# Attention of a hybrid decoder layer: masks behind a step's products, and both branches of a head in a row

## The reference, cut to what matters

```
s = einsum('bgrqd,bgnd->bgrqn', qi, ck) * scale            # compressed keys, 63 blocks
p_c = masked_softmax(s, cmp_end[None, :] <= t[:, None])
...
s = einsum('bgrqd,bgqkd->bgrqk', qi, ksel) * scale         # selected blocks of 64 keys
p_s = masked_softmax(s, smask[:, :, None])                 # key <= token
...
s = einsum('bgrqd,bgkd->bgrqk', qi, kwi) * scale           # window of 512 keys
p_w = masked_softmax(s, wmask)
...
o = gates[..., 0:1] * o_c + gates[..., 1:2] * o_s + gates[..., 2:3] * o_w
```

## Time and profile before

| | |
|---|---|
| median of 3 runs | 1591.72 us (1591.71 to 1593.87) |
| profiled execution | 1593.65 us |
| its span (first to last instruction) | 1591.9 us, 1.75 outside it |
| mean granted TensorE clock | 0.991 of 2.4 GHz |
| attention, about | 366 to 652 us of the span |
| of it token tiles 0 to 3 (steps 0 to 7) | 366.0 to 468.7 us |

### The profile page before, as it was taken

The page is one execution under the profiler, slowest core; times in us unless marked ns, Lnnn a source line. Parts: engine busy times, 40 slices in busy tenths (PEclk is TensorE's granted clock), DMA queues, the critical chain, the costliest instruction groups (busy, mean ns, idle before and its releaser), DMA issues.

```text
span 1591.9 us, 21511 instructions
## 1 busy us (share of the span) xinstructions
PE 1556.8 (98%) x8238; PEld 1264.0 (79%) x8238; DVE 894.6 (56%) x1561; ACT 536.8 (34%) x936; POOL 78.4 (5%) x126
## 2 busy tenths in 40 slices
PE   7999999998999999999999999999999999999997
PEld 6888888897666666788888888888888888888885
DVE  7832455446777777443455555656555555556332
ACT  6112222246677777422222211222112221223221
POOL 0111222220000000000000000000000000000000
PEclk9999999998999999999999999999999999999998
DMA  6433243380000000601211111121111111122011
GB/s 229 134 105 127 93 146 102 111 261 18 24 18 14 15 1 15 237 1 44 76 40 60 59 40 40 40 79 40 40 40 57 62 40 40 40 80 106 27 40 40
DMA packets 53239, 110.57 MB, mean 69 GB/s; under 512 B 13104, under 2 KB 22320, under 8 KB 53168
## 3 DMA queue, kind: packets, MB, share of 16 engines
q1 hardware_dynamic: 45744, 85.47, 16.2%
q0 software_dynamic: 7424, 24.12, 4.5%
HBM read 89.65 MB, written 19.92 MB: 69 GB/s over the span
## 4 chain that ended last, share of the span: by engine, by line
PE 95%; DVE 2%; issue 2%; ACT 1%; DMA 0%; DVEq 0%; POOLq 0%; POOL 0%; SPq 0%; ACTq 0%
PE ps L1521 29%; PE ps L1140 15%; PE ps L1142 15%; PE ps L1141 15%; PE ps L1247 6%; PE ps L1426 5%; PE ps L1383 3%; PE ps L1384 2%; PE ps L1508 1%; PE ps L1292 1%; PE ps L1240 1%; PE ps L1145 1%; PE ps L1387 1%; PE ps L1206 1%; PE ps L1381 0%
## 5 line engine op out<-in xcount | busy, mean ns | idle before, releaser
L2070 DVE TENSOR_TENSOR h<-h,ps 128x512 f32<-128x512 f32 x336 | 224.3, 686 | 137.9 <-PE ps L1142 136.2
L1521 PE MATMUL ps<-hth,wuh 128*128 128x512 f32 x672 | 206.9, 389 | 0.0
L1521 PE MATMUL ps<-htl,wuh 128*128 128x512 f32 x672 | 206.9, 389 | 0.0
L1521 PE MATMUL ps<-hth,wul 128*128 128x512 f32 x672 | 206.8, 389 | 0.0
L1140 PE MATMUL ps<-wh,xth 128*128 128x512 f32 (+1 forms) x448 | 175.4, 392 | 8.0 <-DVE wl L1655 8.0
L1142 PE MATMUL ps<-wh,xtl 128*128 128x512 f32 (+1 forms) x448 | 169.4, 378 | 0.0
L1141 PE MATMUL ps<-wl,xth 128*128 128x512 f32 (+1 forms) x448 | 168.9, 377 | 0.0
L1521 PEld LDWEIGHTS ps<-htl,wuh 128*128 128x128 f32 x672 | 126.1, 188 | 26.2
L1521 PEld LDWEIGHTS ps<-hth,wuh 128*128 128x128 f32 x672 | 126.1, 188 | 26.2
L1521 PEld LDWEIGHTS ps<-hth,wul 128*128 128x128 f32 x672 | 126.1, 188 | 26.2
L1084 ACT ACTIVATE ffh<-ffa 128x1024 fp32r<-128x1024 f32 x22 | 23.3, 1061 | 358.3 <-DVE ffa L2097 358.3
(11 more groups left out here) (249 smaller groups left out, 2593.0 us busy)
## 6 DMA issues: line engine op xcount, KB each, us to landing
wuraw<-in_w_up SPq DMA_DIRECT2D x44, 512.0 KB, 5.1
wraw<-in_w_in SPq DMA_DIRECT2D x48, 256.0 KB, 3.4
proj_d<-stage POOLq DMA_DIRECT2D x48, 256.0 KB, 2.3
wdraw<-in_w_down SPq DMA_DIRECT2D x22, 512.0 KB, 3.5
rin<-proj_d POOLq DMA_DIRECT2D x20, 256.0 KB, 4.6
xraw<-in_xt SPq DMA_DIRECT2D x16, 256.0 KB, 5.6
owraw<-in_w_out SPq DMA_DIRECT2D x8, 512.0 KB, 5.8
h<-in_x SPq DMA_DIRECT2D x1, 4096.0 KB, 16.8
```

The source lines that it names most:

```text
L1521: mm = nc.tensor.matmul(ps[:, 2 * part + half, :], w_, x_[:, k, half * 512:(half + 1) * 512], start=(k == 0 and i == 0), stop=(k == NK - 1 ...
L2070: nc.vector.tensor_tensor(hh, hh, ps[:, 4 + o_ % 4, :], ALU.add).then_inc(dn_add, 1)
```

## The change

1. The row of products and masks is split in two functions: `qk_products` issues all products of a unit, `qk_masks` behind them the masks. In tiles 4 to 7 the far mask thus comes behind the joint products, with the diagonal and the compressed mask.
2. In tiles 0 to 3 (`late`, `paired`) PE computes both branches of a head in a row in every second slot: products of both, then masks of both (`qk_pair`). The DVE takes both row maxima at the start of the even slot, ACT both exponentials at the end of the odd slot.
3. In these tiles, which need one bank a unit, units use two sets of banks: selected scores bank 0 or 1, window scores bank 2 or 3, by the head's parity (`score_bank`). A unit waits for exponentials four units back (`apart`). Unit 1 waits for those of the whole step before (its compressed scores use bank 3), unit 3 for `csub_done` of its own step.
4. For steps 0 to 7 the transposes, outputs and `close` start one slot later; for steps 6 and 7 they are packed in 7 slots, so that they end where they ended.

```diff
+        def late(v):
+            return v < G * WIN_T
+        def paired(v):
+            return late(v)
...
-                base = per * (v + 1) + 1
+                base = per * (v + 1) + (2 if late(v) else 1)
+                span = per - 1 if late(v) and not late(v + 2) else per
...
-                    slots[base + per * at // total].extend(unit)
+                    slots[base + span * at // total].extend(unit)
...
-                slots[base + per - 1].append(("close", v))
+                slots[base + span - 1].append(("close", v))
...
+        def apart(t):
+            return 4 if t < WIN_T else 2
+        def score_bank(t, i):
+            r_, br = divmod(i, 2)
+            return 2 * br + (r_ % 2 if t < WIN_T else 0)
...
+            def exp_places(n, length):
+                v, i = divmod(n, 2 * RG)
...
+                if late(v):
+                    return {length: [i - 1, i]} if i % 2 else {}
+                if not paired(v):
+                    return {length: [i]}
...
-            def qk(v, i):
+            def qk_products(v, i):
...
-                if n >= 2:
+                if n >= apart(t):
+                    pe.wait_ge(exp_done, n - apart(t) + 1)
+                if i == 1 and t < WIN_T and n >= 2:
                     pe.wait_ge(exp_done, n - 1)
                 if i == 1 and v:
                     pe.wait_ge(csub_done, CSUB0 + v)
+                if i == 3 and t < WIN_T:
+                    pe.wait_ge(csub_done, CSUB0 + v + 1)
+                if i == 2 and v == 0:
+                    pe.wait_ge(cvc_done, CVC0 + 1)
...
+            def qk_masks(v, i):
+                t, (r_, br) = v // G, divmod(i, 2)
+                far = br and t >= WIN_T
+                at = (t - (max(0, t - WIN_T) if br else 0)) * P
+                if far:
+                    nc.tensor.matmul(ps[:, 2, 0:P], ident_b[:], far_b, start=False, stop=True)
+                mm = nc.tensor.matmul(ps[:, score_bank(t, i) + at // 512, at % 512:at % 512 + P], ident_b[:], diag_b,
+                                      start=False, stop=not far)
+                if far:
+                    c0 = P + r_ * HD
+                    mm = nc.tensor.matmul(ps[:, 3, c0:c0 + HD], ident_b[:], cmp_b[:, t], start=False, stop=True)
                 mm.then_inc(qk_done, 1)
+            def qk(v, i):
+                qk_products(v, i)
+                qk_masks(v, i)
+            def qk_pair(v, r_):
+                for br in range(2):
+                    qk_products(v, 2 * r_ + br)
+                for br in range(2):
+                    qk_masks(v, 2 * r_ + br)
...
-            qk(0, 0)
+            qk_pair(0, 0)
...
-                if n + 1 < 2 * RG * NV:
-                    qk(*divmod(n + 1, 2 * RG))
+                v_, i = divmod(n + 1, 2 * RG)
+                if v_ < NV and not paired(v_):
+                    qk(v_, i)
+                elif v_ < NV and i % 2 == 0:
+                    qk_pair(v_, i // 2)
...
-                if n < 2 * RG * NV:
-                    row_max(*divmod(n, 2 * RG))
+                u_, i = divmod(n, 2 * RG)
+                if u_ < NV and not paired(u_):
+                    row_max(u_, i)
+                elif u_ < NV and i % 2 == 0:
+                    row_max(u_, i)
+                    row_max(u_, i + 1)
```

More of the change, by code:

```diff
@@ L939, in exponentials @@
                     act.wait_ge(tr_full, turns_of["turn_p", v - 2, len(key_tiles(v - 2)) - 1] + 1)
-                s_, pr = ps[:, 2 * br:2 * br + 2, :].rearrange("p a n -> p (a n)"), prob[:, v % 2, r_]
+                at = score_bank(t, i)
+                s_, pr = ps[:, at:at + 2, :].rearrange("p a n -> p (a n)"), prob[:, v % 2, r_]
                 m, q = n % 4, n // 2 % 4
@@ L981, in nsa_high @@
                                      ps[:, 7, 0:2 * P].rearrange("p (a n) -> p a n", a=2), ACT.Copy).then_inc(nsah_done, 1)
+            def exp_places(n, length):
+                v, i = divmod(n, 2 * RG)
+                if v >= NV:
+                    return {}
+                if late(v):
+                    return {length: [i - 1, i]} if i % 2 else {}
+                if not paired(v):
+                    return {length: [i]}
+                if i % 2:
+                    return {}
+                if i == 0:
+                    return {length: [0, 1]}
+                return {(length + 1) // 2: [i], length: [i + 1]} if length > 1 else {length: [i, i + 1]}
             for e in range(2):
@@ L1006, in _ @@
             for n, slot in enumerate(slots):
-                for st in slot:
+                at_ = exp_places(n, len(slot))
+                for m, st in enumerate([*slot, ("end",)]):
+                    for i in at_.get(m, ()):
+                        exponentials(n // (2 * RG), i)
                     {"split_q": q_split_high, "turn_q": q_turned, "turn_p": p_high, "turn_ret": ret_high,
                      "close": nsa_high}.get(st[0], skip)(st)
-                if n < 2 * RG * NV:
-                    exponentials(*divmod(n, 2 * RG))
                 if n in OW_SLOTS:
@@ L1366, in qk @@
                     w = min(512, width - c)
-                    bank = 2 * br + c // 512
+                    bank = score_bank(t, i) + c // 512
                     at = w0 * P + c
[L1369 to L1375, removed]
+                    if br and c:
                         two = ps[:, 3:5, :].rearrange("p a n -> p (a n)")[:, 0:2 * c0].rearrange("p (b n) -> p b n", b=2)[:, :, 0:P]
@@ L1380, in qk @@
                             pair = bass.AP(k_, first, [[CK + 3 * HD, P], [gap, 2], [1, P]])
-                            mm = nc.tensor.matmul(two, q_, pair, start=k_ is keys_s, stop=False)
+                            nc.tensor.matmul(two, q_, pair, start=k_ is keys_s, stop=False)
                     else:
+                        ends = c + w < width and not br
                         nc.tensor.matmul(ps[:, bank, 0:w], q_, aks[:, br, g_, at:at + w], start=True, stop=False)
[L1384 to L1389, removed]
+                        nc.tensor.matmul(ps[:, bank, 0:w], q_, akx[:, br, g_, at:at + w], start=False, stop=ends)
                 if i == 1 and t < WIN_T:
@@ L1395, in qk @@
                         nc.tensor.matmul(sc_, qc, ckx[:, g_ * NCMP:g_ * NCMP + HD], start=False, stop=False)
-                        mm = nc.tensor.matmul(sc_, ident_b[:], cmp_b[:, t], start=False, stop=True)
-                mm.then_inc(qk_done, 1)
+                        nc.tensor.matmul(sc_, ident_b[:], cmp_b[:, t], start=False, stop=True)
+            def qk_masks(v, i):
[9 more added lines that the diff above has]
+                    mm = nc.tensor.matmul(ps[:, 3, c0:c0 + HD], ident_b[:], cmp_b[:, t], start=False, stop=True)
+                mm.then_inc(qk_done, 1)
+            def qk(v, i):
[6 more added lines that the diff above has]
+                    qk_masks(v, 2 * r_ + br)
             def p_turn(st):
@@ L1891, in row_max @@
                 m = n % 4
-                s_ = ps[:, 2 * br:2 * br + 2, :].rearrange("p a n -> p (a n)")
+                at = score_bank(t, i)
+                s_ = ps[:, at:at + 2, :].rearrange("p a n -> p (a n)")
                 if br == 0:
@@ L1900, in row_max @@
                 c_ = cmpst[:, v % 2]
-                scores = s_[:, 5 * P:5 * P + RG * HD].rearrange("p (r n) -> p r n", r=RG)[:, :, 0:NCMP]
+                scores = ps[:, 3, P:P + RG * HD].rearrange("p (r n) -> p r n", r=RG)[:, :, 0:NCMP]
                 maximum = mark(nc.vector.reduce_max(c_[:, C_MAX], scores, AX_X, negate=True))
```

## The result

The changed kernel takes 1599.70 us at the median of 22 executions (1593.67 to 1601.61), the kernel before 1593.47 us (22 executions, 1590.67 to 1595.33): ratio 1.0032, 95% interval 1.0024 to 1.0041 (the ratios here weigh all executions and lie near the quotient of the means, not of the medians). It is **slower by 0.3%**; the forecast was 1591.0 us and the range ended at 1598.0.

The account below looks back on a forecast made before the run. TensorE, busy 98% of the span, was taken as the bound. Terms -2.3 (steps 0 to 7) + 3.0 (clock) + 0.5 (step 8) - 2.0 (masks) = -0.8 us from 1591.72 gave 1591.0 us, range 1584.5 to 1598.

Parts of the forecast that it names:

- One sign of being wrong: Listed as refuting: steps 6 and 7 not longer, clock in steps 4 to 7 below 1.00, tiles 4 to 7 changing over 3 us.
- One sign of being right: Listed as confirming, among others: steps 0 to 3 shorter by 3 us or more together.
- Wait A: Step's head: head 0's window product waits for all exponentials of the step before; PE stands 1.8 us in step 7.
- Wait B: Head 1's window product waits for the compressed maximum's subtraction: 0.3 us in steps 6 and 7, about 1.6 in 3 to 5.
- Steps 4 to 7: Token tiles 2 and 3, one step per head group: 61.0 against 57.4 us, 3.6 us lost at full clock.
- Steps 0 to 3: Token tiles 0 and 1, DVE sets the pace: 39.4 against 45.3 us, 5.9 won, 3 given back to the clock.
- Step 8's head: Later transposes take 1.6 us of cover from step 8's start: 0.5 us lost, bounds 0 and 1.6.
- Masks last in tiles 4 to 7: Far mask behind the joint products hides 0.08 us of weight load per head: 2.0 us won, bounds 0 and 2.6.
- That holds at 2.4 GHz throughout: Assumption behind the net 2.3 us won in steps 0 to 7; only steps 0 to 3 got a clock correction, 3 us.
- the third rival: Holes at PE pull the clock down in steps 4 to 7: 9 us lost, 1600; if half, 1596; chance 0.22.
- the cases without it: Gains given back (0.38), denser early steps keep the clock (0.35), window-exponential wait at step heads costs nothing new (0.05).
- point of decision: The clock loss in steps 4 to 7 decides once a second low-clock stretch appears, each some 2 us.

Follow-up runs that it names:

- holes_filled: Changed kernel with selected products repeated on PE ahead of the four long waits in steps 4 to 7; 1591.90 us, ratio 0.9989.
- masks_only: Changed kernel with only the masks behind the products kept; no pairs, second set of banks or later slot; 1591.31 us, ratio 0.9994.
- t01_filled: Changed kernel with pairs in token tiles 0 and 1 alone, plus repeated products in the holes of steps 0 to 3; 1589.02 us, ratio 0.9971.
- pairs_t01: Changed kernel with pairs, two sets of banks and later transposes in token tiles 0 and 1 alone; 1590.66 us, ratio 0.9983.
- t01_shift: `pairs_t01` with four repeats of the first unit's products at the head of attention; 1591.47 us, ratio 0.9987.
- shift_1us: Changed kernel with four repeats of the products at attention's very first unit, 0.9 us later; 1601.90 us, ratio 1.0058.
- shift_2us: Changed kernel with eight repeats of the products at attention's very first unit, 1.2 us later; 1602.35 us, ratio 1.0060.
- no_later: Changed kernel with start and spread of the transposes, outputs and close as before the change; 1606.65 us, ratio 1.0089.
- mask_first: Changed kernel with head 0 of a step not paired, its mask right behind its selected products; 1597.25 us, ratio 1.0017.

## Why the prediction was wrong

Forecast 1591.0 us, measured 1599.70, and slower, which had a chance of 0.28. Of the 8.7 us between, 1.75 were in the start: the forecast began at 1591.72, the median of three executions, and 22 give 1593.47 for the same kernel. Beside that the time moved by +6.2 us instead of -0.8. One sign of being wrong stood in the first profile already: a clock below 1.00 in steps 4 to 7 (0.87 in step 4). One sign of being right was missing: steps 0 to 3 won 1.2 us, not 3 or more. Step by step, by the profiles:

- **Wait A**: 1.8 us in step 7 and 1.6 in step 6 were forecast, 1.75 and 1.53 came. Right.
- **Wait B**: 1.7 and 1.6 us in steps 4 and 5 were forecast, 1.61 and 1.60 came; in steps 6 and 7, where 0.3 was forecast, no wait of its kind shows. In step 3 1.6 was forecast and 1.45 came. Right.
- **Steps 4 to 7**: 12.25, 13.3, 15.45 and 20.0 us were forecast, 13.3, 12.6, 14.9 and 19.4 came: 61.0 against 60.2 us. That this is near is in part luck. The forecast was for a clock of 1.00, and step 4's low stretch is in the 60.2. In `holes_filled`, at 1.00, these steps take 58.5 us (409.87 to 468.42). The written order was priced some 2.5 us too high.
- **Steps 0 to 3**: 5.9 - 3.0 = 2.9 us won forecast, 1.2 measured. The clock is the suspect: the forecast took 3 us for 18 us at the low level, 0.17 each. The changed kernel has 0.77 over 44.1 us, 20 us at the low level, and `masks_only` against before suggests 0.32 each, 6.4 us. That is too much to fit (39.4 + 6.4 = 45.8, measured 44.1). `t01_filled` against `pairs_t01` gives at least 1.6 us for some 10 us, 0.16 each, with the repeats' own work in it. How the 1.7 us too few divide between the clock and the written order isn't shown.
- **Step 8's head**: 0.5 forecast, 0.4 measured (a wait of 1.02 us, as written out). Right.
- **Masks last in tiles 4 to 7**: 2.0 forecast, 1.7 measured, and 0.12 us between the joint products as forecast. The row of 0.20 beside 0.12 us spoke rightly.
- **The step that failed** is the clock in steps 4 to 7 ("That holds at 2.4 GHz throughout"). The forecast's sum took it as 1.00 there, on the ground of rows 2 (step 4 with PE idle 2 of 13.1 us at 1.00). Instead 3.2 to 10 us at 1.2 GHz follow waits A and B, and without these holes the time is 1591.9 us instead of 1599.70. That idle time was in pieces: the longest wait of PE from 410 to 470.5 us before is 0.9 us, in `t01_shift` 1.1 us, and both keep 1.00. Less idle time, but in one piece of 1.6 us, did not keep it in step 4 of the changed kernel. The piece alone isn't the whole rule: before, in steps 0 to 3, 20 us ran at the low level with no wait over 0.9 us. I had written down the pieces' length, and the third rival with it, and still weighed the share of idle time more: 0.22 for the rival against 0.78 for the cases without it.

What the rival said of its size: 9 us, or half of it, 1596 to 1600. The groups are some 6 us apart. The low stretches shown are 3.2 to 6.6 us long in `shift_1us` and 10 us in `shift_2us`. By the 1.6 us that 3.5 us cost in step 4, that is an estimate of 1.5 to 4.6 us each; I had put some 2. Its point of decision, "from the point where a second such stretch appears", fits too: the first group has one in step 4 and takes 1594.

The Trainium skill's page "TensorE: Matmul & The Clock Gate", section "A second HAM failure mode: psum-queue depth-cycling", on short idle times between groups of matmuls that make the clock swing, was named against this change. The rows of `shift_1us` agree with it: 0.50 behind holes of 1.53 to 1.74 us, 1.00 between. The page adds that its kernel's median matmul had its full-clock time and puts the loss in falling and rising again between the bursts; here it is the windows behind a hole that are at 0.50.

**Still open** is what decides in which group an execution of the same file falls, why in its shorter group the three later holes leave the clock alone, and what sets the length of a low stretch (a hole of 1.75 us had 10 us behind it in `shift_2us`, holes of 2.4 to 2.8 us had some 3 in `no_later`). A shift of 0.9 us turned all executions into the long kind, so it hangs on fractions of a microsecond in time; more was not tried. The kernel before isn't free of it: its 22 executions spread over 4.7 us. That its spread comes from steps 0 to 3 is argued from the clocks there (0.77 in its profile, 0.84 in that of `masks_only`), not shown.

## What to carry to other kernels

Where PE is nearly the bound, ask of a new wait not only how long it is but whether it is one piece: no wait of up to 1.1 us was followed by a low clock in steps 4 to 7, while behind those of 1.2 to 1.8 us up to 10 us ran at 1.2 GHz, at a price of about half their length. A profile of one execution can miss such a cost; compare the median's distance with the profile's, look at the mean clock of every run, and shift the stage by a microsecond to bring it out. Where a hole can't be scheduled away, repeating a harmless product in it may be cheaper than the hole, and a change can be kept to the tiles where it does no harm: with pairs in tiles 0 and 1 alone the kernel takes 1590.7 us, with pairs in tiles 2 and 3 too 1599.7.

## What the runs showed that I had not expected

- More products made kernels faster: 1600 to 1591.9 us with 14 repeated pairs of products in steps 4 to 7, 1590.7 to 1589.0 with 24 in steps 0 to 3.
- Added work of 0.9 us at one place cost 2.2 us at the median (1599.7 to 1601.9), because it made all executions long: the long group itself went from some 1600.8 to 1601.9.
- One core and one file gave two groups of executions some 6 us apart, at 0.985 and 0.989 in mean clock for the changed kernel, 0.986 and 0.991 for `mask_first`.
